# Gated scan in 128-key score products, up-projection loads behind the last input block, heads in another order

## What is computed

```
b = jnp.cumsum(gc, axis=1)                      # log gates of a chunk
b_ref = b[:, CHUNK // 2 - 1][:, None]
o_inter = einsum('bchk,bhkv->bchv', qc * exp(b), S)
A = einsum('bthk,bshk->bhts', qc * exp(b - b_ref), kc * exp(b_ref - b))
A = where(mask, A, 0.0)                         # mask: key not after query
o_intra = einsum('bhts,bshv->bthv', A, vc)
S_new = exp(b_last)[..., None] * S + einsum('bshk,bshv->bhkv', kc * exp(b_last - b), vc)
```

## Time and profile before

| | |
|---|---|
| median of 3 runs | 2609.93 us (2604.38 to 2614.36) |
| span of the profiled execution, first to last instruction | 2608.0 us |
| TensorE busy | 2469.2 us, 95% |
| VectorE, ScalarE, GpSimd busy | 51%, 31%, 34% |
| mean granted TensorE clock | 0.963 |

### The profile page before, as it was taken

How to read it: one execution, slowest core, us unless ns; L and a number is a source line. 1 busy time by engine, 2 the same in 40 slices (tenths; PEclk the granted TensorE clock), 3 DMA queues, 4 the chain that set the end, 5 groups by cost and what they waited for, 6 DMA issues and landing times.

```text
span 2608.0 us, 30893 instructions
## 1 busy us (share of the span) xinstructions
PE 2469.2 (95%) x13081; PEld 2036.7 (78%) x13081; DVE 1334.8 (51%) x1717; ACT 798.4 (31%) x1088; POOL 880.5 (34%) x633
## 2 busy tenths in 40 slices
PE   7999899999999999898999999989999888999998
PEld 4888778888888888688777778878887447888886
DVE  2898764645444344876666655564542424211113
ACT  2322761311111112336632222234342433322213
POOL 2006002233233232453034555534342003444442
PEclk9898999999999999899999999989998999999999
DMA  8232103224343332222044555521103001233331
GB/s 269 91 98 83 65 1 114 81 81 129 122 135 93 120 103 84 73 82 66 1 113 142 149 158 153 182 89 50 49 17 113 17 0 49 74 105 94 92 97 57
DMA packets 309225, 240.57 MB, mean 92 GB/s; under 512 B 10692, under 2 KB 304831, under 8 KB 309087
## 3 DMA queue, kind: packets, MB, share of 16 engines
q1 hardware_dynamic: 308674, 238.47, 30.0%
q10 hardware_dynamic: 414, 0.13, 0.0%
HBM read 232.29 MB, written 2.10 MB: 90 GB/s over the span
## 4 chain that ended last, share of the span: by engine, by line
PE 85%; DVE 9%; ACT 4%; DMA 1%; issue 1%; POOL 0%; SPq 0%; DVEq 0%; ACTq 0%
PE ps L2538 62%; PE ps L1161 5%; PE ps L2573 2%; DVE mod_w L2170 2%; PE ps L947 2%; DVE mod_ctx L2170 1%; PE ps L1181 1%; PE ps L734 1%; PE ps L2490 1%; PE ps L685 1%; PE ps L761 1%; PE ps L1204 1%; PE ps L909 1%; DVE small L1051 1%; PE ps L2453 1%
## 5 line engine op out<-in xcount | busy, mean ns | idle before, releaser
L1676 POOL TENSOR_TENSOR w_lo<-raw,w_hi 128x512 fp32r<-128x512 f32 x518 | 755.3, 1488 | 1395.7 <-ACT w_hi L1784 1395.7
L2538 PE MATMUL ps<-h_hi,w_hi 128*128 128x512 f32 x1994 | 650.8, 372 | 26.2 <-DVE h_lo L2134 22.1
L2538 PE MATMUL ps<-h_lo,w_hi 128*128 128x512 f32 x1994 | 640.4, 367 | 0.0
L2538 PE MATMUL ps<-h_hi,w_lo 128*128 128x512 f32 x1994 | 640.0, 367 | 0.0
L1784 ACT ACTIVATE w_hi<-raw 128x2048 fp32r<-128x2048 f32 (+2 forms) x155 | 264.7, 1708 | 601.3 <-PE ps L2538 372.9
L2538 PEld LDWEIGHTS ps<-h_hi,w_hi 128*128 128x128 f32 x1994 | 341.3, 191 | 95.9 <-issue 23.3
L2538 PEld LDWEIGHTS ps<-h_hi,w_lo 128*128 128x128 f32 x1994 | 340.6, 190 | 67.2
L2538 PEld LDWEIGHTS ps<-h_lo,w_hi 128*128 128x128 f32 x1994 | 341.1, 191 | 66.0 <-issue 0.2
L2061 ACT ACTIVATE xg<-ps 128x512 f32<-128x512 f32 (+1 forms) x66 | 44.2, 670 | 679.0 <-PE ps L2538 492.2
L2170 DVE SCALAR_TENSOR_TENSOR mod_w<-mod_w,cond 128x512 f32<-128x512 f32 x224 | 241.7, 1079 | 3.4
L2538 PE MATMUL ps<-hid_hi,w_hi 128*128 128x512 f32 x704 | 231.7, 370 | 0.0
(11 more groups left out here) (376 smaller groups left out, 3259.0 us busy)
## 6 DMA issues: line engine op xcount, KB each, us to landing
mod_w<-in_w_mod SPq DMA_DIRECT2D x72, 1024.0 KB, 9.7
raw<-in_w_ffn_in SPq DMA_DIRECT2D x88, 512.0 KB, 5.2
raw<-in_w_in SPq DMA_DIRECT2D x54, 512.0 KB, 4.8
raw<-in_w_ffn_out SPq DMA_DIRECT2D x48, 384.0 KB, 3.8
raw<-in_w_out SPq DMA_DIRECT2D x24, 512.0 KB, 4.6
raw<-in_w_gate SPq DMA_DIRECT2D x22, 512.0 KB, 4.0
raw<-in_w_up SPq DMA_DIRECT2D x22, 512.0 KB, 5.3
raw<-in_w_down SPq DMA_DIRECT2D x24, 384.0 KB, 3.5
```

The costliest lines, as they stand in the source:

```text
L1676: ins = pool.tensor_tensor(w_lo[:, s, at:end], raw[:, s, at:end], w_hi[:, s, at:end].bitcast(F32), ALU.subtract)
L2538: ins = pe.matmul(ps[0:m, at:at + tw], weight(part, k, cols), v[:, held[k] if held else k, t0:t0 + tw], start=(at_k == 0 and j == 0 and no ...
```

## The change

Three parts, all in layer 2. The scores: the late queries of two chunks are multiplied in one product with all 128 keys of both (64 query columns in two strips), written side by side to 512 PSUM columns; the early ones stay as they were but for their place, and follow all late ones. One masked copy of 128 partitions takes the place of two of 64; its mask also leaves out keys of the other chunk. The loads: `w_uq`, `w_ukv` and `rot` follow the load of block 13, with a semaphore of its own for `w_ukv`. The order: queries of heads 1, 2, 3, 0 and keys of heads 3, 2, 0, 1, in all engines' programs alike, and the values' places in PSUM follow the keys'.

```diff
@@ SyncE
                     if l == 2 and b == B_HG + 2:
-                        sp.wait_ge(g_b, ED)
-                        sp.wait_ge(g_turned, ED - 1)
-                        sp.dma_start(rot[:, :, :], a["rot_b"]).then_inc(rot_in, 16)
-                    if l == 2 and b == B_HG:
                         sp.wait_ge(g_b, ED)
                         sp.wait_ge(l_ss, 1)
...
-                            sp.dma_start(w_ukv[:, k, :], a["w_ukv_2"][0][k * P:(k + 1) * P, :]).then_inc(uq_in, 16)
+                        for k in range(2):
+                            sp.dma_start(w_ukv[:, k, :], a["w_ukv_2"][0][k * P:(k + 1) * P, :]).then_inc(ukv_in, 16)
+                        sp.wait_ge(g_turned, ED - 1)
+                        sp.dma_start(rot[:, :, :], a["rot_b"]).then_inc(rot_in, 16)
@@ TensorE
+        Q_ORDER, K_ORDER = (1, 2, 3, 0), (3, 2, 0, 1)
...
                 early, late = (0, mid) if d == 0 else (mid, 0)
+                for t in range(LAT // P):
+                    to = ps[:, A_AT + P * t:A_AT + P * t + P].rearrange("p (c s) -> p c s", s=CHUNK)
+                    queries = at_token(g_q2[d], P * t, P).rearrange("p (c s) -> p c s", s=CHUNK)
+                    pe.matmul(to[:, :, late:late + mid], at_token(g_k[d], P * t, P), queries[:, :, late:late + mid],
+                              start=True, stop=True)
                 for c in range(NCH_LAT):
-                    row, at = CHUNK * (c % 2), A_AT + CHUNK * (c // 2)
-                    for q0, k0, kw in ((late, 0, CHUNK), (early, early, mid)):
-                        ins = pe.matmul(ps[row + k0:row + k0 + kw, at + q0:at + q0 + mid],
-                                        at_token(g_k[d], CHUNK * c + k0, kw), at_token(g_q2[d], CHUNK * c + q0, mid),
-                                        start=True, stop=True)
+                    row, at = CHUNK * (c % 2) + early, A_AT + CHUNK * c + early
+                    ins = pe.matmul(ps[row:row + mid, at:at + mid], at_token(g_k[d], CHUNK * c + early, mid),
+                                    at_token(g_q2[d], CHUNK * c + early, mid), start=True, stop=True)
                 ins.then_inc(g_a, 1)
...
-            pe.wait_ge(uq_in, 96)
-            for h in range(HEADS):
+            pe.wait_ge(uq_in, 64)
+            for h in Q_ORDER:
                 if h == 0:
                     pe.wait_ge(in_free, first_piece(14))
...
+            pe.wait_ge(ukv_in, 32)
             pe.wait_ge(l_norm, 1)
-            for h in range(HEADS):
+            for h in K_ORDER:
                 if h < 2:
                     pe.wait_ge(l_turned, h + 1)
                 elif h == 2:
                     pe.wait_ge(l_norm, 2)
@@ VectorE
-                for hf in range(2):
-                    rows, cols = slice(CHUNK * hf, CHUNK * hf + CHUNK), slice(CHUNK * hf, CHUNK * hf + CHUNK)
-                    at = (C_MF, C_MB)[d] + CHUNK * hf
-                    mask = const[rows, at:at + CHUNK].bitcast(I32).unsqueeze(1).to_broadcast([CHUNK, 4, CHUNK])
-                    ins = dve.copy_predicated(g_masked[rows, d, :].rearrange("p (t s) -> p t s", s=P)[:, :, cols], mask,
-                                              ps[rows, A_AT:A_AT + 256].rearrange("p (t s) -> p t s", s=CHUNK))
-                ins.then_inc(g_am, 1)
+                at = (C_MF, C_MB)[d]
+                mask = const[:, at:at + P].bitcast(I32).unsqueeze(1).to_broadcast([P, LAT // P, P])
+                dve.copy_predicated(g_masked[:, d, :].rearrange("p (t s) -> p t s", s=P), mask,
+                                    ps[:, A_AT:A_AT + LAT].rearrange("p (t s) -> p t s", s=P)).then_inc(g_am, 1)
```

More of the change, by code:

```diff
@@ L410, in program @@
         l_spread, l_wide = sem("l_spread"), sem("l_wide")
-        uq_in, m_f, ctx2_landed = sem("uq_in"), sem("m_f"), sem("ctx2_landed")
+        uq_in, ukv_in, m_f, ctx2_landed = sem("uq_in"), sem("ukv_in"), sem("m_f"), sem("ctx2_landed")
         in_tile, in_free = sem("in_tile"), sem("in_free")
@@ L1318, in last_layer_pe @@
                     cols = w_ukv[:, k, :].rearrange("p (h n) -> p h n", n=256)[:, :, P:256]
-                    ins = pe.matmul(ps[:, 1024 * (t % 4):1024 * (t % 4) + 512], ckv[:, k, P * t:P * t + P], cols,
+                    at = 1024 * K_ORDER[t % 4]
+                    ins = pe.matmul(ps[:, at:at + 512], ckv[:, k, P * t:P * t + P], cols,
                                     start=(k == 0), stop=(k == 1))
@@ L1454, in last_layer_act @@
             next_hi(base_in[2] + B_HG + 2)
-            for h in range(HEADS):
-                act.wait_ge(l_up, h + 1)
+            for i, h in enumerate(Q_ORDER):
+                act.wait_ge(l_up, i + 1)
                 act.activation(qn_hi[:, h, :], ps[:, Q_AT[h]:Q_AT[h] + LAT], ACT.Copy, scale=q_scale).then_inc(l_taken, 1)
@@ L1469, in last_layer_act @@
                 act.activation(q_turn[own, h, :], q_rope[own, h // 2, :], ACT.Copy).then_inc(l_high, 1)
-            for h in range(HEADS):
-                act.wait_ge(l_up, 9 + h)
+            for i, h in enumerate(K_ORDER):
+                act.wait_ge(l_up, 9 + i)
                 act.activation(kn_hi[:, h, :], ps[:, 1024 * h:1024 * h + TOK], ACT.Copy).then_inc(l_taken, 1)
@@ L1474, in last_layer_act @@
                 act.wait_ge(l_up, 13 + t)
-                act.activation(v_l[:, t, :], ps[:, 1024 * (t % 4):1024 * (t % 4) + 512], ACT.Copy).then_inc(l_taken, 1)
+                at = 1024 * K_ORDER[t % 4]
+                act.activation(v_l[:, t, :], ps[:, at:at + 512], ACT.Copy).then_inc(l_taken, 1)
             attention_act(act, 2, lambda u: o_mla[:, u["h"], :])
@@ L1591, in last_layer_dve @@
             spread(dve, l_root, n_root[:, 4:10], TOK // P).then_inc(l_spread, 1)
-            for h in range(HEADS):
-                dve.wait_ge(l_taken, h + 1)
+            for i, h in enumerate(Q_ORDER):
+                dve.wait_ge(l_taken, i + 1)
                 dve.scalar_tensor_tensor(qn_lo(h), halves(ps[:, Q_AT[h]:Q_AT[h] + LAT]), q_scale,
@@ L1622, in last_layer_dve @@
                                   ).then_inc(l_low, 1)
-            for h in range(HEADS):
-                dve.wait_ge(l_taken, 7 + h)
+            for i, h in enumerate(K_ORDER):
+                dve.wait_ge(l_taken, 7 + i)
                 dve.tensor_tensor(kn_lo[:, h, :], ps[:, 1024 * h:1024 * h + TOK], kn_hi[:, h, :].bitcast(F32), ALU.subtract
```

## The result

The changed kernel takes 2574.66 us (median of 4 runs, 2572.57 to 2577.28), the one before 2608.58 (4 runs, 2604.38 to 2614.36). The ratio is 0.987, with a 95% interval from 0.9857 to 0.9883: 33.9 us less, where 26.7 were forecast. The range began at 2575.0, so the time lies 0.3 us outside, on the fast side. The profiled span fell by 32.5 us, from 2608.0 to 2575.5.

What follows compares the result with a forecast made beforehand. The prediction took TensorE, busy 95% of the span, as the bound. Its terms 10.4 + 4.8 + 5.5 + 0.8 + 5.2 = 26.7 us, taken from 2609.9, gave 2583 us, range 2575 to 2596.

Steps and rivals of the forecast that it cites:

- What bounds the kernel: Whole kernel: TensorE, busy 95% of the span; an edit pays by shortening its work or its waits.
- Part 1, the scores: Scan's score stages: fewer passes and form changes save 1.3 us in each of 8, 10.4 us; ends 6.0 and 11.8.
- I take 0.067 a pass: Small score products: assumed price of each of 16 passes, 1.07 us a stage, leaving room for alternating array places.
- the lower bound of a small pass: Small score products: 0.03 us for the load plus 0.027 for the queries, 0.057 a pass.
- Part 1b, the clock: After key stages in the scan: three of four half-clock stretches go, 1.6 us each, 4.8 us; bounds 0 and 6.4.
- Part 2, the loads: Weight blocks after the scan: earlier loads remove a 4.14 us wait and slow passes, 5.5 us; bounds 3.5 and 6.5.
- C: Blocks after the scan and values: new waits halve the clock again, 7.5 in place of 11.5; 2587 us, chance 0.10.
- E: Moved loads: an overlooked wait keeps B_HG+1 from coming earlier, 5.5 us lost; 2589 us, chance 0.05.
- Part 3, the heads: Query and key products: new orders remove waits, 0.8 us at the queries and 5.2 us at the keys.
- A: Score stages: a small product costs 0.205 us whatever stands beside it; 2591 us, chance 0.22.
- B: Clock: slow stretches stay as many, coming with other sparse passes too, 4.8 us lost; 2588 us, chance 0.12.
- D: Score stages: 128-key products reading queries in two strips lose load overlap, making it slower; 2613 us, chance 0.02.

Runs made afterwards that it cites:

- e5: The kernel of e1 with the even chunks of each group ahead of the odd ones, so neighbouring products share a place of the array: 2591.1 us (one run).
- e6: The changed kernel with each 128-key score product followed at once by its own two small 32-key ones: 2586.03 us (one run).
- e1: The kernel before with only its score products reordered, all 64-key ones first, then all 32-key ones: 2590.98 us, ratio 0.991.
- e11: The kernel of e8 run once more, beside e10: 2575.63 us, ratio 0.9873.
- e3: The kernel before with only the up-projection and rotation-table loads moved behind the load of block 13: 2606.35 us, ratio 0.9973.
- e4: The kernel before with only the new orders of query and key heads: 2605.39 us, ratio 0.997.
- e9: The changed kernel with scores and masks put back as before, keeping the new loads and orders of heads: 2596.85 us, ratio 0.9957.
- e7: The changed kernel with the early small products of every stage made eight times over: 2598.22 us (one run).
- e2: The kernel before with only the changed scores (128-key products) and the one masked copy: 2591.24 us, ratio 0.992.
- e8: The changed kernel with the four 128-key products of a stage replaced by eight of 64 keys by 32 queries: 2576.17 us, ratio 0.9868.
- e10: The changed kernel run once more, for comparison with e11 on the same chip: 2576.24 us, ratio 0.9875.

## Why the prediction came out as it did

*What bounds the kernel.* Right: all the time came from TensorE's own work in the scan and from the waits of rows 4; behind attention nothing changed (546.01 and 546.07 us).

*Part 1, the scores.* This is the step that failed, in the term "I take 0.067 a pass". The stage saves 1.97 us, not 1.3: 15.8 us in all for 10.4, and more than the upper end of 11.8. The direction was read rightly from rows 6 and 7: it is the change of form that costs, and e5 and e6 show it. What was wrong is the lower bound of a small pass, 0.03 for its load plus 0.027 for its queries, one after the other. They overlap: with neighbours in one place a 32-column pass takes 0.032 (e5), about the 0.03 of its load alone; with neighbours in alternating places 0.024, where the passes of two products start 0.006 us apart. A row of the trace before already showed such an overlap: 22 passes of 64*128 in 1.60 us, 0.07 each, against 0.11 for the 128*128 passes in rows 7. It was used as a landmark only, not as a price.

The rule cited there, that a change of tiling mode drains TensorE (the Trainium skill, TensorEngine Tiling (Array Packing), Key Properties), fits e6, where a change costs 0.13 us; that it is a drain which takes this time, no row shows. The same section of the Trainium skill says that different tiles can load and multiply in parallel; e1 against e5 agrees, with 0.96 us against 1.36. I had weighed only the first half of it.

*Part 1b, the clock.* Mis-sized: four slow stretches went, not three. The first stretch of the table fell by 22.4 us, of which 15.8 are the stages: 6.6 for 4.8. Some 0.7 of the 6.6 isn't clock, but the change of form at the start of a stage (0.09 us, e11), which the 128-key version hasn't and which was in no term; that leaves about 1.5 a slow stretch, near the 1.6 taken from rows 8. Part of this is luck: e3, e4 and e9 left the stages as they were, and their profiles have three slow stretches in the scan, not four. e7 shows that length alone doesn't bring them: stages nearly as long, but dense, were followed by none. e6 shows none behind passes in changing form in a shorter stage. What of the two counts for how much stays open. Two terms of the sum, then, part 1 by 5.4 us and part 1b by 1.8, make up the 7.2 us by which the forecast fell short.

*Part 2, the loads.* Right, step by step: 5.4 us for 5.5, a wait of 0.94 for 1.05 ahead of B_HG+2, no slow stretch behind it, no wait on the moved loads (e3 alone gives the same). Rivals C and E are out.

*Part 3, the heads.* Right: 0.94 for 0.8 and 5.05 for 5.2 us, and VectorE's first key remainder is what the values wait for (0.31 us).

*Rivals.* A is out: the position does matter, but alternating it makes a stage shorter (0.96 us against 1.36), not longer. B is out for the scan; the latent sums kept their slow stretch, as B said of them. D is out: strips cost nothing (8 passes in 0.93 us).

*The range.* Its low end was made of bounds that were taken for firm. The bound of the small pass had no row of its own, so it should have been lower; a row of overlapped passes was there to set it. That the time fell just outside is chance: it is 0.3 us below 2575.0, and the median of the kernel before moved by 1.4 us between the three runs of the forecast and the four of the result. The 5.4 us of part 1 are not chance.

## What to carry to other kernels

Order small products by the number of their weight columns before thinking about making them larger: e1's swap of two loops brought as much as the new product, its mask and its layout (0.991 and 0.992). Count the change of form at the start of such a run too (e11). Let neighbours go to alternating places of the array. When a stage ahead of a late load becomes shorter, part of its gain turns into waiting for that load, so a wait in the queue that holds a prefetch back is to be moved in the same step.

## What the runs showed of the hardware

A change of the weight form between two f32 products cost 0.13 to 0.14 us (e6, e5), and 0.09 at the entry from 128 to 64 columns (e11). Eight f32 products of 128 by 32 by 32, in two places in turn, took 0.38 us, 16 passes. In the scan of before the granted clock fell to 0.5 four times, and in those of e3, e4 and e9 three times, each within 1 us of the end of a run of products in changing form that lasted 3.28 us or a little more. In the changed kernel and in e1, e2, e5, e6, e7, e8, e10 and e11 it never did so up to 1956 us, with runs from 0.96 to 3.08 us. What the chip counts was not measured.
